# Attention stage: the low parts of q and k and the high and low parts of v are made by VectorE instead of GpSimd

## The chip, the cores and the metric

The kernel runs on one core of a Trainium2 chip. The metric is the device time of one launch in microseconds (us), as the median of several runs. Engines are named as the profile names them: PE is TensorE, PEld its weight loads, DVE is VectorE, ACT is ScalarE, POOL is GpSimd, and SP is SyncE, which issues most of the transfers.

## What is computed

One layer of a hybrid encoder, once for a prompt of 1024 tokens and once for 32 sample tokens with a cache of 512 past tokens. The change lies in the attention branch alone:

```python
q, k, v, fl, ga, u, gs = jnp.split(z, [...], axis=-1)         # z = RMSNorm(h) @ w_in
s = jnp.einsum('bthd,bshd->bhts', q, k) * (HEAD_DIM ** -0.5)  # 8 heads of 128
bias = cq[..., :, None] - ck_t[:, :, None, :]                 # cumulated log forget gates
s = jnp.where(kpos <= qpos, s + bias, NEG_INF)
pr = jax.nn.softmax(s, axis=-1)
att = jnp.einsum('bhts,bshd->bthd', pr, v)
mixed = jnp.concatenate([att * silu(ga), ssm * silu(gs)], axis=-1)
h = h + mixed @ w_out
```

All of it is fp32. The kernel makes each fp32 product from three products of rounded parts: a number x is split into a high part (a copy to a rounded type, `F32R`) and a low part (x minus the high part), and high*high, low*high and high*low are accumulated.

## The kernel before

The program is a row of stages, each a block in which the five engines run their own instruction streams and meet only at semaphores: a projection stage, `stage_attention`, a side stage (gated unit and layer embedding), and a post stage with the output projections. No scheduler is at work: each engine executes its stream in the order in which the code was written, and a wait holds all that stands behind it on that engine.

In `stage_attention` the 8 heads come one after the other; heads 0, 1, 6 and 7 are written out, and 2 to 5 run in a loop of two heads a turn. A head has 8 steps. `SLOTS[s]` says which 128-row block of queries a step works on: step 0 has the blocks 0 and 1 (128 and 256 keys), steps 1 to 6 the blocks with 384, 512, 640, 768, 896 and 1024 keys, and step 7 the sample tokens with 544 keys. The chain of one step is:

- PE makes the scores (`scores`, lines 1971 and 2020) into one of two PSUM buffers, two steps ahead of the rest;
- DVE adds the bias and takes the row bound (`bias`, line 2246) into one of four buffers `prob`;
- ACT takes the exponential (`exponentials`, line 2150);
- PE turns the probabilities (`turn_probs`, line 2037; the sample step 2042) into one of two PSUM banks `turned`;
- ACT rounds them to `pt_hi` (`high_parts`, line 2161), and DVE subtracts to get `pt_lo` (`low_parts`, line 2270);
- PE multiplies with v (`weigh`, into `att`, line 1971): queries 0 to 511 at step 5 of the head, queries 512 to 1023 in two halves at step 7 and at step 0 of the next head, the samples at its step 1;
- DVE multiplies `att` with the gate (`gate_out`, line 2280), and a head later with the reciprocal sums (`scale`, line 2262).

In step s of its stream DVE does `bias(s+1)`, then `low_parts(s-1)`, then what else is due: `gate_out` of the last head at steps 1 and 2, `gate_out` of this head at step 6, and at step 7 `low_kc` of the next head, `invert` and `scale`. PE in step s does `scores(s+2)`, one group of transposes for the next head (`turn`, into the one bank `prep`, which ACT copies out by `copy_k`, `copy_v` and `split_kc`), `turn_probs(s)`, and a `weigh` where one is due. Before line 2037 may write a bank, `lo_done` of the group that used this bank last must be there; before a `weigh`, `lo_done` of the last two groups of its queries.

Beside this each head needs its operands in high and low parts, made one head ahead into one of two buffers each. ACT makes `q_hi` and `k_hi` (`split_qk`, line 2119, steps 0 and 1) and `kc_hi`. GpSimd makes the rest in `prepare`, in this order: `k_lo`, `q_lo`, `vc_hi` and `vc_lo` (the cached v), and, once ACT has copied the turned v, `v_hi` and `v_lo`. For head 0 this runs once ahead of everything; for head h+1 it starts when PE has finished the last `weigh` of head h-1 (`weighed[2]`), early in head h.

```python
def prepare(h, b):                      # on GpSimd
    pool.wait_ge(k_hi_done, h + 1)
    sub(k_lo[b][:], k_raw[:], k_hi[b][:], k_lo_done)
    ...
    nc.gpsimd.tensor_copy(v_hi[b][:], v_tok[:]).then_inc(v_hi_done, 1)
    pool.wait_ge(v_hi_done, h + 1)
    sub(v_lo[b][:], v_tok[:], v_hi[b][:], v_lo_done)
```

The semaphores that `prepare` raises are waited for at few places: PE waits for `q_lo_done` and `k_lo_done` ahead of the first scores of a head and for `v_lo_done` ahead of its first `weigh`; ACT waits for `v_lo_done` before it overwrites `v_tok`; SP waits for `k_lo_done`, `q_lo_done`, `vc_hi_done` and `vc_lo_done` before it loads the next `k_raw`, `q_raw`, `kc_raw` and `vc_raw` over the old.

Of the kernel before, what the change touches and what calls it, by code (L numbers as in the profile page):

```python
# [22 lines left out]
F32 = mybir.dt.float32  # L23
# [131 lines left out]
def settle(eng, passed):  # L155

    eng.sem_inc(passed, 1)
# [1596 lines left out]
def stage_attention(nc, d, G):  # L1754
# [15 lines left out]
    with ExitStack() as ctx:  # L1770
# [4 lines left out]
        q_raw, k_raw, v_raw = G["first_raw"]  # L1775
# [61 lines left out]
        def heads(eng, head):  # L1837

            head(0, 0, 0, first=True)
            head(1, 1, 0)  # L1840
            with eng.Fori(1, HEADS // 2 - 1) as i:
                head(i * 2, 0, i)
                head(i * 2 + 1, 1, i)
            head(HEADS - 2, 0, HEADS // 2 - 1)
            head(HEADS - 1, 1, HEADS // 2 - 1, last=True)
# [70 lines left out]
        @block.gpsimd  # L1916
        def _(pool):
            nc.gpsimd.memset(mask_f[:], 0.0)
            nc.gpsimd.memset(mask_s_f[:], 0.0).then_inc(masks_made, 1)
            pool.wait_ge(masks_made, 1)  # L1920

            nc.gpsimd.affine_select(out=mask_f[:], in_=mask_f[:], compare_op=ALU.is_ge, fill=NEG, base=0,
                                    pattern=[[-1, P]], channel_multiplier=1).then_inc(masks_made, 1)
            pool.wait_ge(masks_made, 2)

            r0 = P - T_SAMPLE
            nc.gpsimd.affine_select(out=mask_s_f[r0:], in_=mask_s_f[r0:], compare_op=ALU.is_ge, fill=NEG,
                                    base=0, pattern=[[-1, T_SAMPLE]], channel_multiplier=1) \
                .then_inc(masks_made, 1)
            pool.wait_ge(masks_made, 3)  # L1930
            nc.gpsimd.memset(v_tok[:, TT], 0.0)
            nc.gpsimd.tensor_copy(mask[:], mask_f[:])
            nc.gpsimd.tensor_copy(mask_s[:], mask_s_f[:])
            nc.gpsimd.tensor_copy(ident_bf[:], ident[:]).then_inc(masks_ready, 1)

            def sub(out, a, hi, done):
                nc.gpsimd.tensor_tensor(out, a, hi.bitcast(F32), ALU.subtract).then_inc(done, 1)

            def prepare(h, b):

                pool.wait_ge(k_hi_done, h + 1)
                sub(k_lo[b][:], k_raw[:], k_hi[b][:], k_lo_done)
                pool.wait_ge(q_hi_done, h + 1)
                sub(q_lo[b][:], q_raw[:], q_hi[b][:], q_lo_done)
                pool.wait_ge(c_loaded, h * 32 + 32)
                settle(pool, G["passed"])
                nc.gpsimd.tensor_copy(vc_hi[b][:], vc_raw[:]).then_inc(vc_hi_done, 1)
                pool.wait_ge(vc_hi_done, h + 1)
                sub(vc_lo[b][:], vc_raw[:], vc_hi[b][:], vc_lo_done)
                pool.wait_ge(v_copied, h * 3 + 3)  # L1950
                settle(pool, G["passed"])
                nc.gpsimd.tensor_copy(v_hi[b][:], v_tok[:]).then_inc(v_hi_done, 1)
                pool.wait_ge(v_hi_done, h + 1)
                sub(v_lo[b][:], v_tok[:], v_hi[b][:], v_lo_done)

            prepare(0, 0)

            def head(h, b, i, first=False, last=False):
                if not first:

                    pool.wait_ge(weighed[2], h)
                if not last:
                    prepare(h + 1, 1 - b)
            heads(pool, head)

        @block.tensor
        def _(pe):
            def three(out, pairs, start, stop, lhs, rhs):
# [257 lines left out]
        @block.vector  # L2226
        def _(dve):
            def low_kc(h, b):
                dve.wait_ge(kc_hi_done, h + 1)
                nc.vector.tensor_tensor(kc_lo[b][:], prep[:], kc_hi[b][:].bitcast(F32), ALU.subtract) \  # L2230
                    .then_inc(kc_lo_done, 1)

            def bias(h, s, hb, pair):

                b, it = s % 2, h * 4 + s // 2
                dve.wait_ge(scored[b], it + 1)
                if not isinstance(h, int) or it:
                    dve.wait_ge(exped[b], it)
                if not isinstance(h, int) or it > 1:
                    dve.wait_ge(prob_free[b], h * 4 + (s // 2 - 1))  # L2240
                if s == 0:
                    dve.wait_ge(negc_loaded[hb], pair * 16 + 16)
                settle(dve, G["passed"])
                for n, (t, col) in enumerate(SLOTS[s]):
                    width, row = ((t + 1) * P, 0) if t < TT else (NS, T_PROMPT)
                    z = nc.vector.tensor_tensor_reduce(  # L2246
                        out=prob[s % 4][:, col:col + width], in0=score[b][:, col:col + width],
                        in1=negc[hb][:, row:row + width], scale=-SCALE, scalar=3.0e38, op0=ALU.add, op1=ALU.min,
                        accum_out=stat[b][:, n, 0:1])
                z.then_inc(biased[b], 1)  # L2250

            def invert(h, hb):
                for b in range(2):
                    dve.wait_ge(exped[b], h * 4 + 4)
                if not isinstance(h, int) or h > 1:
                    dve.wait_ge(rec_turned, h - 1)
                nc.vector.reciprocal(rec[hb][:], sums[hb][:]).then_inc(rec_ready, 1)

            def scale(h, hb):
                dve.wait_ge(gated, h * 3 + 3)  # L2260
                dve.wait_ge(rec_loaded, h * 32 + 32)
                nc.vector.tensor_tensor(mix[hb][:], mix[hb][:], rec_bc[:], ALU.mult).then_inc(scaled, 1)

            def low_parts(h, s):
                for n, group in enumerate(GROUPS_OF[s]):
                    gi = first_group[s] + n
                    bank, x = turned[gi % 2], (0 if s < 3 else 1 if s < 7 else 2)
                    dve.wait_ge(hi_done[gi % 2], h * (per_head // 2) + (gi // 2 + 1))
                    for (out, src), (hi, _) in zip(taken(group, pt_lo[x], bank), taken(group, pt_hi[x], bank)):
                        c = nc.vector.tensor_tensor(out, src, hi.bitcast(F32), ALU.subtract)  # L2270
                    c.then_inc(lo_done[gi % 2], 1)

            def gate_out(h, x, hb, pair=None):
                cols = slice(512 * x, 512 * x + (512 if x < 2 else T_SAMPLE))
                dve.wait_ge(weighed[x], h + 1)
                if x == 0:
                    if not isinstance(pair, int) or pair:
                        dve.wait_ge(mix_stored[hb], pair * 16)
                    dve.wait_ge(gate_loaded[hb], pair * 16 + 16)
                nc.vector.tensor_tensor(mix[hb][:, cols], att[:, 0:cols.stop - cols.start], gate[hb][:, cols],  # L2280
                                        ALU.mult).then_inc(gated, 1)

            dve.wait_ge(masks_ready, 1)
            low_kc(0, 0)
            bias(0, 0, 0, 0)

            def head(h, hb, i, first=False, last=False):
                for s in range(8):
                    if s < 7:
                        bias(h, s + 1, hb, i)  # L2290
                    elif not last:
                        bias(h + 1, 0, 1 - hb, i + hb)
                    if first and s == 1:
                        for n in range(4):
                            dve.wait_ge(G["sem"][f"z_put{n}"], put_count(2 * NP - 1))
                    if s > 0:
                        low_parts(h, s - 1)
                    elif not first:
                        low_parts(h - 1, 7)
                    if s == 1 and not first:  # L2300
                        gate_out(h - 1, 1, 1 - hb)
                    if s == 2 and not first:
                        gate_out(h - 1, 2, 1 - hb)
                    if not last and s == 7:
                        low_kc(h + 1, 1 - hb)
                    if s == 6:
                        gate_out(h, 0, hb, i)
                    if s == 7:
                        invert(h, hb)
                        if not first:  # L2310
                            scale(h - 1, 1 - hb)
            heads(dve, head)
            low_parts(HEADS - 1, 7)
            gate_out(HEADS - 1, 1, 1)
            gate_out(HEADS - 1, 2, 1)
            scale(HEADS - 1, 1)
# [676 lines left out]
```

## Time and profile before

| | |
|---|---|
| median of 3 runs | 2404.68 us (2404.39 to 2406.39) |
| the profiled execution: its own time, its span | 2403.17 us, 2401.5 us |
| busy over the span: PE, PEld, DVE, ACT, POOL | 93%, 88%, 64%, 33%, 11% |
| granted TensorE clock, mean | 0.979 of full speed |
| attention stage | about 1192 to 1415 us of the span |

The trace gives for each instruction its start and its length, and in brackets how long its engine had sat idle just before it and which instruction on which engine released it. Lengths of neighbours can overlap by a few hundredths of a us, since an engine starts the next instruction while the last one drains. An idle time costs something only if an engine that sets the end waits behind it. The view of stretches gives the busy time of each engine between two moments.

### The profile page before, as it was taken

What the parts mean: (1) busy time and instruction counts of PE and PEld (TensorE: products, weight loads), DVE (VectorE), ACT (ScalarE), POOL (GpSimd) and SP (SyncE); (2) the same over time, 40 slices, a digit from 0 to 9 for tenths busy, and PEclk for the clock granted to TensorE, in tenths of its full rate; (3) what the DMA queues carried; (4) which work ended last, traced back from release to release, by engine and by line L of the source; (5) the groups of instructions that cost most, each with busy time, mean ns of one, the idle gap of its engine ahead of it and who ended that gap; (6) DMA issues with size and microseconds to landing.
All of it is one profiled execution on the core that took longest, in us unless ns stands there. A gap on an engine that the chain in (4) does not pass through costs nothing. (4 is left out here: it accounts for less than half of the span.)

```text
span 2401.5 us, 43214 instructions
## 1 busy us (share of the span) xinstructions
PE 2240.1 (93%) x15969; PEld 2114.6 (88%) x15969; DVE 1539.9 (64%) x2827; ACT 791.0 (33%) x1669; POOL 274.4 (11%) x334
## 2 busy tenths in 40 slices
PE   3999999999899999999799978979999999999996
PEld 3999999999899999999778868967888879999996
DVE  6778766766787788886356646654446666445554
ACT  6542333333533333334366636220001112001112
POOL 0011000000111111211244400000001110001110
PEclk9999999999999999999899989989999999999998
DMA  8484444444757878875376655454445436443442
GB/s 243 147 255 110 141 136 124 150 132 130 283 179 206 237 213 228 232 223 169 124 234 203 200 181 181 127 166 127 114 145 147 113 106 217 111 111 112 110 111 96
DMA packets 401861, 394.65 MB, mean 164 GB/s; under 512 B 75248, under 2 KB 343128, under 8 KB 395248
## 3 DMA queue, kind: packets, MB, share of 16 engines
q1 hardware_dynamic: 353344, 267.24, 38.8%
q0 software_dynamic: 20704, 77.95, 9.8%
q10 hardware_dynamic: 27664, 47.49, 6.1%
q8 instruction: 92, 1.51, 0.3%
q14 instruction: 57, 0.47, 0.1%
HBM read 261.88 MB, written 122.05 MB: 160 GB/s over the span
## 5 line engine op out<-in xcount | busy, mean ns | idle before, releaser
L758 PE MATMUL acc<-t_act,w_hi 128*128 128x264 f32 x5376 | 887.8, 287 | 12.0 <-ACT acc L979 4.1
L758 PEld LDWEIGHTS acc<-t_act,w_hi 128*128 128x128 f32 x5376 | 748.3, 189 | 18.7 <-issue 17.3
L758 PE MATMUL acc<-t_act,w_lo 128*128 128x264 f32 x2688 | 548.3, 285 | 0.0
L2700 PE MATMUL post_acc<-region_hi,w_post_hi 128*128 128x272 f32 (+1 forms) x1536 | 418.0, 326 | 24.3 <-DVE region_lo L2809 19.6
L758 PEld LDWEIGHTS acc<-t_act,w_lo 128*128 128x128 f32 x2688 | 417.4, 189 | 0.0
L2700 PE MATMUL post_acc<-region_hi,w_post_lo 128*128 128x272 f32 (+1 forms) x1536 | 415.0, 324 | 0.0
L2700 PE MATMUL post_acc<-region_lo,w_post_hi 128*128 128x272 f32 (+1 forms) x1536 | 414.4, 324 | 0.0
L2700 PEld LDWEIGHTS post_acc<-region_hi,w_post_hi 128*128 128x128 f32 x1536 | 257.7, 189 | 50.3 <-issue 16.6
L1313 DVE TENSOR_TENSOR w_lo<-w_raw_f,w_hi 128x512 fp32r<-128x512 f32 x288 | 198.0, 687 | 144.3 <-ACT w_hi L968 144.0
L2700 PEld LDWEIGHTS post_acc<-region_lo,w_post_hi 128*128 128x128 f32 x1536 | 258.0, 189 | 22.1
L2700 PEld LDWEIGHTS post_acc<-region_hi,w_post_lo 128*128 128x128 f32 x1536 | 256.7, 189 | 22.8
L968 ACT CAST w_hi<-w_raw_f 128x512 fp32r<-128x512 f32 x288 | 177.9, 618 | 267.3 <-PE acc L758 245.6
L142 DVE TENSOR_TENSOR w_post_lo<-w_raw,w_post_hi 128x1024 fp32r<-128x1024 f32 x128 | 150.5, 1216 | 0.0
L2817 DVE TENSOR_TENSOR total<-post_acc,side 128x512 f32<-128x512 f32 (+1 forms) x32 | 22.6, 708 | 183.4 <-PE post_acc L2700 183.4
L2740 ACT CAST region_hi<-total 128x512 f32 (+1 forms) x32 | 20.4, 636 | 330.7 <-DVE total L2817 319.0
L137 DVE CAST w_post_hi<-w_raw 128x1024 fp32r<-128x1024 f32 x128 | 114.2, 930 | 9.5 <-DMA w_raw<-in_w_out_dram 8.5
L2835 DVE TENSOR_TENSOR h<-h,gate_sig 128x512 f32<-128x512 f32 (+1 forms) x32 | 22.7, 709 | 117.1 <-ACT gate_sig L2747 117.1
L2754 ACT ACTIVATE junk<-y_ps 128x128 f32<-128x128 f32 (+1 forms) x144 | 37.0, 274 | 174.3 <-PE y_ps L2685 174.3
L2651 POOL TENSOR_TENSOR total<-region_hi,region_lo 128x512 f32 (+3 forms) x32 | 50.3, 1575 | 293.1 <-DVE h L2838 285.0
L649 POOL DMA_DIRECT2D zT<-zb x80 | 43.3, 542 | 345.6 <-DVE zb L1329 147.5
L2246 DVE CUSTOM_DVE_ANT_0 prob<-score,negc_bc 128x128 f32<-128x128 f32 (+8 forms) x72 | 53.5, 752 | 32.8 <-PE score L2020 32.5
L2270 DVE TENSOR_TENSOR pt_lo<-turned,pt_hi 128x512 fp32r<-128x512 f32 (+2 forms) x112 | 52.8, 507 | 28.5 <-ACT pt_hi L2161 27.1
(382 smaller groups left out, 3084.9 us busy)
## 6 DMA issues: line engine op xcount, KB each, us to landing
w_raw_f<-in_w_in_dram SPq DMA_DIRECT2D x96, 512.0 KB, 4.1
w_raw<-in_w_out_dram SPq DMA_DIRECT2D x64, 512.0 KB, 4.8
w_raw<-in_w_pg_dram SPq DMA_DIRECT2D x64, 512.0 KB, 4.7
cT<-zb SPq DMA_DIRECT2D x24, 1056.0 KB, 4.7
zb<-cT POOLq DMA_DIRECT2D x96, 264.0 KB, 6.0
zT<-zb POOLq DMA_DIRECT2D x80, 264.0 KB, 3.6
eT<-e_out ACTq DMA_DIRECT2D x16, 528.0 KB, 3.1
t_act<-tS POOLq DMA_DIRECT2D x7, 1056.0 KB, 10.6
```

The costliest lines, as they stand in the source:

```text
L137: nc.vector.tensor_copy(self.hi[b][:, h * self.kh:(h + 1) * self.kh], self.raw[h][:]) \
L142: nc.vector.tensor_tensor(self.lo[b][:, part], self.raw[h][:], self.hi[b][:, part].bitcast(F32), ALU.subtract).then_inc(self.split[h], 1)
L649: pool.dma_start(d["zT"][row:row + P, tok:tok + HN], zb[b][:, i]).then_inc(z_put[i], 16)
L758: mm = pe.matmul(out[:, c, 0:QN], w[:, k, :], t_act[:, SIDE[r], x, k, c * QN:(c + 1) * QN], start=(opens and k == 0 and m == 0), stop=(k = ...
L968: nc.scalar.copy(w_hi[n % RING_W][:], factor(p, r)).then_inc(hi_done, 1)
L1313: TT_(w_lo[n % RING_W][:], factor(n // 7, n % 7), w_hi[n % RING_W][:].bitcast(F32), ALU.subtract) \
L2246: z = nc.vector.tensor_tensor_reduce(out=prob[s % 4][:, col:col + width], in0=score[b][:, col:col + width], in1=negc[hb][:, row:row + widt ...
L2270: c = nc.vector.tensor_tensor(out, src, hi.bitcast(F32), ALU.subtract)
L2651: nc.gpsimd.tensor_tensor(total[b][:, 0:WIDTH[part]], row(hi, part, m).bitcast(F32), row(lo, part, m).bitcast(F32), ALU.add).then_inc(tota ...
L2700: mm = pe.matmul(acc[b][:, c, 0:width], w[:, k, :], a[region][:, k, start:start + width], start=(k == 0 and n == 0), stop=(k == KD - 1 and ...
L2754: s = nc.scalar.activation(junk[0:rows, t], tr_ps[b][0:rows, t * P:(t + 1) * P], ACT.Square, accum_out=ssq[0:rows, t, bass.ds(m, 1)])
L2835: nc.vector.tensor_tensor(h2[b][:, 0:w], h2[b][:, 0:w], sig[b][:, 0:w], ALU.mult).then_inc(e_gated, 1)
```

## The change

The six operations of `prepare` leave GpSimd and go to VectorE, as four pieces: `low_k`, `low_q`, `split_vc` and `split_v`. GpSimd keeps only the making of the masks. Nothing else is edited; the operands, their buffers and their semaphores are the same.

```diff
-            def prepare(h, b):
-                ...
-            prepare(0, 0)
-
-            def head(h, b, i, first=False, last=False):
-                if not first:
-                    pool.wait_ge(weighed[2], h)
-                if not last:
-                    prepare(h + 1, 1 - b)
-            heads(pool, head)
...
+            def sub(out, a, hi, done):
+                nc.vector.tensor_tensor(out, a, hi.bitcast(F32), ALU.subtract).then_inc(done, 1)
+
+            def low_k(h, b):
+                dve.wait_ge(k_hi_done, h + 1)
+                sub(k_lo[b][:], k_raw[:], k_hi[b][:], k_lo_done)
+
+            def low_q(h, b):
+                dve.wait_ge(q_hi_done, h + 1)
+                sub(q_lo[b][:], q_raw[:], q_hi[b][:], q_lo_done)
+
+            def split_vc(h, b):
+                dve.wait_ge(c_loaded, h * 32 + 32)
+                settle(dve, G["passed"])
+                nc.vector.tensor_copy(vc_hi[b][:], vc_raw[:]).then_inc(vc_hi_done, 1)
+                dve.wait_ge(vc_hi_done, h + 1)
+                sub(vc_lo[b][:], vc_raw[:], vc_hi[b][:], vc_lo_done)
+
+            def split_v(h, b):
+                dve.wait_ge(v_copied, h * 3 + 3)
+                settle(dve, G["passed"])
+                nc.vector.tensor_copy(v_hi[b][:], v_tok[:]).then_inc(v_hi_done, 1)
+                dve.wait_ge(v_hi_done, h + 1)
+                sub(v_lo[b][:], v_tok[:], v_hi[b][:], v_lo_done)
+
             dve.wait_ge(masks_ready, 1)
+            low_k(0, 0)
+            low_q(0, 0)
             low_kc(0, 0)
             bias(0, 0, 0, 0)
+            split_vc(0, 0)
+            split_v(0, 0)
...
                     if s == 2 and not first:
                         gate_out(h - 1, 2, 1 - hb)
+                    if not last:
+                        if s == 2:
+                            if not first:
+                                dve.wait_ge(weighed[2], h)
+                            low_k(h + 1, 1 - hb)
+                        if s == 3:
+                            low_q(h + 1, 1 - hb)
+                        if s == 4:
+                            split_vc(h + 1, 1 - hb)
+                        if s == 6:
+                            split_v(h + 1, 1 - hb)
                     if not last and s == 7:
                         low_kc(h + 1, 1 - hb)
                     if s == 6:
                         gate_out(h, 0, hb, i)
```

How DVE's stream stands at three places, before and after. `ISA prob,stat` is a `bias`, `ISA stat` the reading of its row bound; line numbers of the changed kernel are 30 lower around here.

DVE at the start of the stage, ahead of head 0, before:

```order
L2230 TENSOR_TENSOR kc_lo<-prep,kc_hi 128x512
L2246 ISA prob,stat<-score,negc_bc 128x128
L2246 ISA stat 128x1
L2246 ISA prob,stat<-score,negc_bc 128x256
L2246 ISA stat 128x1
L2246 ISA prob,stat<-score,negc_bc 128x384
```

and after:

```order
L2254 TENSOR_TENSOR k_lo<-k_raw,k_hi 128x1056
L2254 TENSOR_TENSOR q_lo<-q_raw,q_hi 128x1056
L2200 TENSOR_TENSOR kc_lo<-prep,kc_hi 128x512
L2216 ISA prob,stat<-score,negc_bc 128x128
L2216 ISA stat 128x1
L2216 ISA prob,stat<-score,negc_bc 128x256
L2216 ISA stat 128x1
L2267 CAST vc_hi<-vc_raw 128x512
L2254 TENSOR_TENSOR vc_lo<-vc_raw,vc_hi 128x512
L2274 CAST v_hi<-v_tok 128x1152
L2254 TENSOR_TENSOR v_lo<-v_tok,v_hi 128x1152
L2216 ISA prob,stat<-score,negc_bc 128x384
```

Two subtractions now stand ahead of `kc_lo`, and four operations stand between the bias of step 0 and that of step 1.

DVE in a head, from the last `gate_out` of the head before (step 2) to the bias of 1024 keys (step 5), before:

```order
L2280 TENSOR_TENSOR mix<-att,gate 128x32
L2246 ISA prob,stat<-score,negc_bc 128x768
L2246 ISA stat 128x1
L2270 TENSOR_TENSOR pt_lo<-turned,pt_hi 128x4x128
L2246 ISA prob,stat<-score,negc_bc 128x896
L2246 ISA stat 128x1
L2270 TENSOR_TENSOR pt_lo<-turned,pt_hi 128x4x128
L2270 TENSOR_TENSOR pt_lo<-turned,pt_hi 128x128
L2246 ISA prob,stat<-score,negc_bc 128x1024
```

and after:

```order
L2254 TENSOR_TENSOR k_lo<-k_raw,k_hi 128x1056
L2216 ISA prob,stat<-score,negc_bc 128x768
L2216 ISA stat 128x1
L2240 TENSOR_TENSOR pt_lo<-turned,pt_hi 128x4x128
L2254 TENSOR_TENSOR q_lo<-q_raw,q_hi 128x1056
L2216 ISA prob,stat<-score,negc_bc 128x896
L2216 ISA stat 128x1
L2240 TENSOR_TENSOR pt_lo<-turned,pt_hi 128x4x128
L2240 TENSOR_TENSOR pt_lo<-turned,pt_hi 128x128
L2267 CAST vc_hi<-vc_raw 128x512
L2254 TENSOR_TENSOR vc_lo<-vc_raw,vc_hi 128x512
L2216 ISA prob,stat<-score,negc_bc 128x1024
```

Each of the three biases has work for the next head directly ahead of it.

DVE in a head, from the `low_parts` of 896 keys (step 6) to that of 1024 keys (step 7), before:

```order
L2270 TENSOR_TENSOR pt_lo<-turned,pt_hi 128x4x128
L2270 TENSOR_TENSOR pt_lo<-turned,pt_hi 128x3x128
L2280 TENSOR_TENSOR mix<-att,gate 128x512
L2246 ISA prob,stat<-score,negc_bc 128x128
L2246 ISA stat 128x1
L2246 ISA prob,stat<-score,negc_bc 128x256
L2246 ISA stat 128x1
L2270 TENSOR_TENSOR pt_lo<-turned,pt_hi 128x4x128 x2
```

and after:

```order
L2240 TENSOR_TENSOR pt_lo<-turned,pt_hi 128x4x128
L2240 TENSOR_TENSOR pt_lo<-turned,pt_hi 128x3x128
L2274 CAST v_hi<-v_tok 128x1152
L2254 TENSOR_TENSOR v_lo<-v_tok,v_hi 128x1152
L2250 TENSOR_TENSOR mix<-att,gate 128x512
L2216 ISA prob,stat<-score,negc_bc 128x128
L2216 ISA stat 128x1
L2216 ISA prob,stat<-score,negc_bc 128x256
L2216 ISA stat 128x1
L2240 TENSOR_TENSOR pt_lo<-turned,pt_hi 128x4x128 x2
```

The split of v stands ahead of the gate, of the first bias of the next head and of the `low_parts` of 1024 keys.

## Rows read from the trace of the kernel before

**Rows 1.** Stretches, one loop head: length, busy us of each engine, granted clock, DMA
```profile
core 0: us, PE busy (x) PEld busy (x) DVE busy (x) ACT busy (x) POOL busy (x), PEclk, DMA share, GB/s
1315.85:1341.92 26.07, 24.16 (x167) 21.14 (x167) 16.52 (x39) 17.32 (x43) 10.51 (x7) 1.00 0.67 217
```

**Rows 2.** Timeline, DVE in a loop head: start, us, instruction, [idle before <-releaser]
```profile
1315.73 0.19 DVE L2280 TENSOR_TENSOR mix<-att,gate 128x32 f32<-128x32 f32 x1 [0.61 <-PE att L1971]
1317.24 0.96 DVE L2246 CUSTOM_DVE_ANT_0 prob<-score,negc_bc 128x768 f32<-128x768 f32 x1 [1.32 <-PE score L2020]
...
1319.21 1.09 DVE L2246 CUSTOM_DVE_ANT_0 prob<-score,negc_bc 128x896 f32<-128x896 f32 x1 [0.19 <-PE score L2020]
...
1321.15 0.89 DVE L2270 TENSOR_TENSOR pt_lo<-turned,pt_hi 128x512 fp32r<-128x512 f32 x2 [0.84 <-ACT pt_hi L2161]
1322.28 1.23 DVE L2246 CUSTOM_DVE_ANT_0 prob<-score,negc_bc 128x1024 f32<-128x1024 f32 x1 [0.24 <-PE score L2020]
...
1323.59 1.02 DVE L2270 TENSOR_TENSOR pt_lo<-turned,pt_hi 128x512 fp32r<-128x512 f32 x2
1324.53 0.71 DVE L2246 CUSTOM_DVE_ANT_0 prob<-score,negc_bc 128x544 f32<-128x544 f32 x1
...
1326.61 1.16 DVE L2270 TENSOR_TENSOR pt_lo<-turned,pt_hi 128x512 fp32r<-128x512 f32 x2 [1.36 <-ACT pt_hi L2161]
1328.15 0.69 DVE L2280 TENSOR_TENSOR mix<-att,gate 128x512 f32<-128x512 f32 x1 [0.38 <-PE att L1971]
1329.12 0.29 DVE L2246 CUSTOM_DVE_ANT_0 prob<-score,negc_bc 128x128 f32<-128x128 f32 x1 [0.28 <-PE score L2020]
...
1330.35 1.29 DVE L2270 TENSOR_TENSOR pt_lo<-turned,pt_hi 128x512 fp32r<-128x512 f32 x2 [0.58 <-ACT pt_hi L2161]
```

**Rows 3.** Timeline, ACT and PE in the same loop head
```profile
1321.65 1.07 ACT L2150 ACTIVATE prob<-prob,stat 128x896 f32<-128x896 f32 x1
1324.86 1.15 ACT L2150 ACTIVATE prob<-prob,stat 128x1024 f32<-128x1024 f32 x1
1331.77 0.50 PE L1971 MATMUL att<-pt_hi,v_hi 128*128 128x512 f32 x1 [0.19 <-DVE pt_lo L2270]
```

**Rows 4.** Single lines, DVE splits elsewhere: ns min/median/max, first and last start, shape
```profile
L137 DVE CAST w_post_hi<-w_raw x128: 635/686/1861, 1599.2 to 2355.4; 128x1024 fp32r<-128x1024 f32 x128
L137 DVE CAST w_glu_s_hi<-w_glu_s_raw x16: 419/423/440, 1492.0 to 1567.9; 128x512 fp32r<-128x512 f32 x16
L142 DVE TENSOR_TENSOR w_glu_s_lo<-w_glu_s_raw,w_glu_s_hi x16: 682/685/718, 1492.6 to 1568.8; 128x512 fp32r<-128x512 f32 x16
L2493 DVE TENSOR_TENSOR y_lo<-y_raw,y_hi x8: 1251/1252/1259, 1449.8 to 1498.2; - x6, 128x1056 fp32r<-128x1056 f32 x2
```

**Rows 5.** Timeline, start of the stage: DVE, ACT, PE
```profile
1206.83 0.56 DVE L2246 CUSTOM_DVE_ANT_0 prob<-score,negc_bc 128x384 f32<-128x384 f32 x1 [0.52 <-PE score L2020]
...
1207.43 0.62 ACT L2150 ACTIVATE prob<-prob,stat 128x384 f32<-128x384 f32 x1
...
1208.60 0.54 ACT L2161 CAST pt_hi<-turned 128x128 fp32r<-128x128 f32 x2 [0.46 <-PE turned L2037]
...
1210.66 0.66 PE L1990 MATMUL prep<-ident,k_raw 128*128 128x128 f32 x4 [1.03 <-ACT k_tok L2125]
```

**Rows 6.** Timeline, head 0: DVE and ACT
```profile
1218.37 1.23 DVE L2246 CUSTOM_DVE_ANT_0 prob<-score,negc_bc 128x1024 f32<-128x1024 f32 x1 [0.25 <-PE score L2020]
...
1225.82 1.29 DVE L2270 TENSOR_TENSOR pt_lo<-turned,pt_hi 128x512 fp32r<-128x512 f32 x2 [0.67 <-ACT pt_hi L2161]
...
1220.29 1.18 ACT L2150 ACTIVATE prob<-prob,stat 128x1024 f32<-128x1024 f32 x1
```

**Rows 7.** Timeline: DVE casts beside a POOL addition; `k_lo` on POOL; last head's bias
```profile
1817.63 2.38 DVE L137 CAST w_post_hi<-w_raw 128x1024 fp32r<-128x1024 f32 x2
...
1817.92 1.54 POOL L2651 TENSOR_TENSOR total<-region_hi,region_lo 128x512 f32 x1 [10.31 <-DVE h L2838]
...
1315.85 2.47 POOL L1937 TENSOR_TENSOR k_lo<-k_raw,k_hi 128x1056 fp32r<-128x1056 f32 x1 [10.72 <-PE att L1971]
...
1394.26 0.96 DVE L2246 CUSTOM_DVE_ANT_0 prob<-score,negc_bc 128x768 f32<-128x768 f32 x1 [1.31 <-PE score L2020]
```

More of the change, by code:

```diff
@@ L1934, in _ @@
             nc.gpsimd.tensor_copy(ident_bf[:], ident[:]).then_inc(masks_ready, 1)
-            def sub(out, a, hi, done):
-                nc.gpsimd.tensor_tensor(out, a, hi.bitcast(F32), ALU.subtract).then_inc(done, 1)
-            def prepare(h, b):
[L1941 to L1954, printed above, removed]
-            prepare(0, 0)
-            def head(h, b, i, first=False, last=False):
-                if not first:
-                    pool.wait_ge(weighed[2], h)
-                if not last:
-                    prepare(h + 1, 1 - b)
-            heads(pool, head)
         @block.tensor
```

## The prediction

> **What bounds the kernel now.** I read the table of stretches first, one loop head at a time [rows 1]: in 26.07 us PE is busy for 24.16, DVE for 16.52, ACT for 17.32, POOL for 10.51, at the full granted clock. So the stage is PE's, with 1.9 us of PE waits a head, and a faster engine for the splits can give back no more than those. POOL's 10.5 us hide beside PE: nothing in the rows of PE waits for them. What to see next is where DVE's 9.5 us of idle lie, for it is not one hole: from step 2 to step 7 the timeline shows nine small ones of 0.19 to 1.36 us, between operations that other engines wait for [rows 2]. Third, who waits for DVE at once: at step 7 PE starts the weighing of queries 512 to 1023 at 1331.77, released by `pt_lo` [rows 3], whose two operations ended at 1330.35 + 1.29 = 1331.64 [rows 2]. Whatever delays that `low_parts` delays PE one for one. The other places have ACT between DVE and PE, with some margin.
>
> **Prices on DVE.** No split of q, k or v stands on DVE in this trace; the same operations on the same types do elsewhere [rows 4]. A subtraction of 128x1056 takes 1.252 us and one of 128x512 0.685, so 1.04 ns an element, and 1.352 us for the 1152 of `v_lo`. A cast of 512 takes 0.423 and of 1024 0.686 in the median, 0.514 ns an element: 0.752 us for `v_hi`. That is 1.25 + 1.25 + 0.42 + 0.69 + 0.75 + 1.35 = 5.7 us a head, and DVE comes to 22.2 of 26 us. Neighbours on DVE overlap by about 0.08 us (1323.59 + 1.02 = 1324.61, next start 1324.53) [rows 2], which I take off, but not between a high part and its low part, where DVE waits for itself; there I put a gap of 0.05 (an estimate; from no gap to 0.1).
>
> **Start of the stage.** `low_k` and `low_q` of head 0 cost nothing: they fall into the time in which PE and ACT hand each other the turned k and v. `split_vc` and `split_v` do cost. DVE ends the bias of step 0 at 1206.83 - 0.52 = 1206.31 [rows 5] and then does 0.42 + 0.69 + 0.75 + 1.35 with two gaps and two overlaps, to about 1209.4; the bias of step 1 started at 1206.83 [rows 5] and is 2.6 late. ACT's exponential of step 1 started at 1207.43, right behind that bias; it goes to 1210.05. Behind it on ACT stand the first `pt_hi`, which had 0.46 us of idle to give [rows 5], `k_hi` of head 1 and the copy of its turned k, and for that copy PE already waited 1.03 us at 1210.66 [rows 5]. So 2.6 less about 0.5: **+2.1 us** on PE, from 1.5 (no gaps, more slack on ACT) to 2.9.
>
> **Steps 2 to 4 of a head.** `k_lo` takes 1.25 us in the hole of 1.32 ahead of the bias of 768 keys [rows 2]: nothing. `q_lo` pushes the bias of 896 keys from 1319.21 by 0.9; it is done at 1321.2, before ACT takes it up at 1321.65 [rows 3], and the idle of 0.84 ahead of the next `pt_lo` [rows 2] swallows it. `vc_hi` and `vc_lo` (1.1 us less overlap, 0.24 of idle) push the bias of 1024 keys by 0.75, to end at 1324.25; ACT takes it up at 1324.86 [rows 3]: nothing. The `pt_lo` behind it is 0.6 late, the bias of 544 keys too, and the idle of 1.36 at 1326.61 [rows 2] ends it. **0**, with margins of some 0.45 and 0.6 us on ACT.
>
> **Step 6.** From the `pt_lo` at 1326.61 to that at 1330.35 DVE has three holes, 0.38 + 0.28 + 0.58 = 1.24 us [rows 2]. `v_hi` starts at 1327.69 and ends at 1328.44, `v_lo` runs from 1328.49 to 1329.84, the gate from 1329.76 to 1330.45, the two small biases to about 1331.0; `pt_lo` starts there instead of at 1330.35. What was the last thing before (`pt_hi` from ACT, with 0.58 of idle on DVE) is now early, and DVE is last: **+0.6 us** a head on PE, from 0.4 (the gate's own hand-overs overlap more) to 0.9 (no overlap at all). It is paid in heads 1 to 6, since head 7 prepares nothing: 3.6 us, from 2.4 to 5.4. After PE's weighing everything keeps its place relative to PE, so nothing earns it back within the head.
>
> **Head 0** has no `gate_out` of an earlier head, no `scale` and no storing of sums, and ACT runs closer behind DVE there: the exponential of 1024 keys started at 1220.29, 0.69 us after its bias had ended (1218.37 + 1.23 = 1219.60) [rows 6], against 1.35 in a loop head (1324.86 less 1323.51) [rows 2, 3]. The same walk puts that bias 1.3 late relative to the rest, so here exponential, `pt_lo` and PE's transposes are about 1 us late, and the split of v comes on top: the `pt_lo` of 1225.82 with its 0.67 of idle [rows 6] is **1.5 us** late beyond the start's 2.1; from 0.6 (as a loop head) to 2.4.
>
> **Waits and queues.** The new waits of DVE (`k_hi_done`, `q_hi_done`, `c_loaded`, `v_copied`, `weighed[2]`) are all for work that is done when DVE comes by: POOL did each of these operations earlier than or at the place where DVE will do it, save `v_hi`, where ACT's last small copy of v stands before DVE's `pt_lo` ends. Behind each wait stand the biases and `pt_lo`; that is the order that I walked. On SP, the loads of `k_raw`, `q_raw`, `kc_raw` and `vc_raw` wait for the same semaphores; `k_lo` and `q_lo` come no later than before, and the cached v is loaded behind PE's turning of the cached k at step 6 anyway. Those operands are used a head later: 0.
>
> **Sum.** 2.1 + 1.5 + 3.6 = 7.2 us on the profiled execution's 2403.17 (its span of 2401.5 and 1.7 around it) gives 2410.4; the median of the runs lies 1.5 above that execution, so the forecast for the median is **2411.9 us**, +0.3%. The stage ends with all engines meeting, so what is lost in it moves the end.
>
> **Rivals.** All of it hidden but the start. What speaks for it is DVE's idle sum, 9.5 us against 5.7. The place is the hole at step 6: if ACT's `pt_hi` or PE's transposes come 0.6 us later relative to DVE than in the rows, or the split of v takes 1.3 us instead of 2.1, `pt_lo` is again released by ACT and a head costs nothing. Then 2404.7 + 2.1 = 2406.8, and with head 0 too 2408.3; this ends not slower by the bound of 0.2% (4.8 us), which is about what a measurement of this kernel can tell from no change. Against it: the hole is 1.24 us by the rows. 28%.
>
> Faster, since GpSimd lets the memory go. Casts on DVE do suffer beside POOL: a pair that overlaps a POOL addition took 2.38 us [rows 7], against a median of 0.686 each, and the longest single one took 1.861 [rows 4]. If DVE's biases and subtractions in this stage suffered alike, POOL's leaving would shorten them; all of PE's waits being owed to that would give 7 x 1.9 = 13.3, less the start's 2.1, so 2393.5 at the best, and it needs more than half of this to pass 0.2%. Against it: the bias of 768 keys took 0.96 us [rows 2] while POOL made `k_lo` at 1315.85 to 1318.32 [rows 7], and in the last head, where POOL has nothing, also in 0.96 [rows 7]. The stage has no casts on DVE before. 4%. The Trainium skill (GPSIMD Engine Reference, Key points) states that GpSimd shares its SBUF interfaces with VectorE, with contention for instructions in a 2-port mode or with two SBUF inputs. By that rule this change would free DVE; the casts of the post stage agree, and the biases of this stage, with their scores in PSUM, show nothing of it.
>
> Heavier. If DVE hands over slower than I count (gaps of 0.1, no overlap), or casts run at the subtraction's rate (`v_hi` 1.2 instead of 0.75), ACT's margins of 0.45 and 0.6 at steps 3 and 4 are used up and a head costs 1.2 us instead of 0.6: 2.9 + 2.2 + 6 x 1.2 = 12.3, so 2417.0. The 1.861 in the row of casts speaks for it, but it stands beside POOL work that is gone here. 10%.
>
> That the change does something else than it says is excluded by the order of instructions: POOL has no arithmetic left in the heads, and DVE has six operations more for each.
>
> **How the numbers follow.** The forecast (a cost above 4.8 and below 11) gets 58%, hidden 28%, heavier 10%, faster 4%. Slower by over 0.2%: 58 + 10 = 68%; within 0.2%: 28%; faster: 4%. The range reaches down to the start alone, 2406.8, and up to the heavier case at 2417.0, with half a us on each side.
>
> **What would show it.** In the new trace: POOL without a row between the masks and the side stage; the bias of step 1 some 2.6 us after the bias of step 0 instead of 0.6; about 26.7 us from head to head instead of 26.07, with PE's busy time unchanged at 24.2; at step 7 a PE wait of some 0.8 us released by `pt_lo`, and that `pt_lo` without idle ahead of it; unchanged intervals in steps 2 to 5. `v_hi` near 0.75 us and `v_lo` near 1.35. Heads of 26.07 us would prove the step 6 term wrong; waits of ACT for `stat` at steps 4 and 5 would prove the margins wrong; shorter biases or `pt_lo` would be the memory rival.

## The result and the profile after

The changed kernel takes 2412.28 us (median of 9 runs, 2408.78 to 2413.64) against 2404.83 of the kernel before (9 runs), a ratio of 1.0028 with a 95% interval of 1.0019 to 1.0037: 7.45 us slower by the two medians, where 7.2 were forecast. The profiled execution after took 2412.7 us, its span is 2411.0.

The page's first lines and the stretch of one loop head, from step 2 to step 2, which answers to [rows 1]:

```profile
PE 2244.7 (93%) x15969; PEld 2118.3 (88%) x15969; DVE 1578.8 (65%) x2875; ACT 792.0 (33%) x1669; POOL 190.4 (8%) x286
```
```profile
1321.68:1348.28 26.60, 24.16 (x167) 21.12 (x167) 21.30 (x44) 17.42 (x43) 0.00 (x0) 1.00 0.70 213
```

PE and ACT do the same work as before; POOL's 10.51 us became 4.8 us more of busy time on DVE (the six rows sum to 5.7 us, as priced; where neighbours overlap, busy time counts the moment once), and the head is 0.53 us longer. DVE in that head, answering to [rows 2] (start, us, instruction, idle before it):

```profile
1321.79 1.25 DVE L2254 TENSOR_TENSOR k_lo<-k_raw,k_hi 128x1056 fp32r<-128x1056 f32 x1
1323.20 0.96 DVE L2216 CUSTOM_DVE_ANT_0 prob<-score,negc_bc 128x768 f32<-128x768 f32 x1 [0.17 <-PE score L1990]
...
1324.89 1.25 DVE L2254 TENSOR_TENSOR q_lo<-q_raw,q_hi 128x1056 fp32r<-128x1056 f32 x1
...
1327.11 0.89 DVE L2240 TENSOR_TENSOR pt_lo<-turned,pt_hi 128x512 fp32r<-128x512 f32 x2
...
1328.97 1.22 DVE L2216 CUSTOM_DVE_ANT_0 prob<-score,negc_bc 128x1024 f32<-128x1024 f32 x1
...
1332.58 1.16 DVE L2240 TENSOR_TENSOR pt_lo<-turned,pt_hi 128x512 fp32r<-128x512 f32 x2 [0.81 <-ACT pt_hi L2131]
1333.65 0.75 DVE L2274 CAST v_hi<-v_tok 128x1152 fp32r<-128x1152 f32 x1
1334.43 1.36 DVE L2254 TENSOR_TENSOR v_lo<-v_tok,v_hi 128x1152 fp32r<-128x1152 f32 x1
1335.71 0.68 DVE L2250 TENSOR_TENSOR mix<-att,gate 128x512 f32<-128x512 f32 x1
...
1336.86 1.28 DVE L2240 TENSOR_TENSOR pt_lo<-turned,pt_hi 128x512 fp32r<-128x512 f32 x2
```

`k_lo` leaves 0.17 us of the hole of 1.32. Behind `q_lo` and the cached v DVE runs without a pause until 0.81 us of the hole of 1.36 are still there at 1332.58: up to that point the head is as before. From there to the last `pt_lo` it is 4.28 us, 3.74 before, without any idle. PE right behind (its waits at step 7; first the one of the kernel before at the same place), and ACT's two exponentials of steps 4 and 5, 3.23 us apart as before (3.21 in [rows 3]):

```profile
1331.14 0.43 PE L2042 MATMUL turned<-ident,prob 32*128 32x32 f32 x5 [0.41 <-issue]
```
```profile
1337.65 0.43 PE L2012 MATMUL turned<-ident,prob 32*128 32x32 f32 x5 [0.96 <-issue]
1338.28 0.50 PE L1941 MATMUL att<-pt_hi,v_hi 128*128 128x512 f32 x1 [0.20 <-DVE pt_lo L2240]
```
```profile
1327.60 1.07 ACT L2120 ACTIVATE prob<-prob,stat 128x896 f32<-128x896 f32 x1
...
1330.83 1.15 ACT L2120 ACTIVATE prob<-prob,stat 128x1024 f32<-128x1024 f32 x1
```

The start of the stage, answering to [rows 5], DVE, ACT and PE:

```profile
1207.45 0.42 DVE L2267 CAST vc_hi<-vc_raw 128x512 fp32r<-128x512 f32 x1
...
1210.58 0.55 DVE L2216 CUSTOM_DVE_ANT_0 prob<-score,negc_bc 128x384 f32<-128x384 f32 x1
...
1211.17 0.62 ACT L2120 ACTIVATE prob<-prob,stat 128x384 f32<-128x384 f32 x1 [2.62 <-DVE stat L2216]
1211.19 0.50 PE L1941 MATMUL score<-k_hi,q_hi 128*128 128x512 f32 x1 [1.34 <-DVE stat L2216]
...
1213.82 0.66 PE L1960 MATMUL prep<-ident,k_raw 128*128 128x128 f32 x4 [1.29 <-ACT k_tok L2095]
```

To compare stages I use PE's own rows: the *start* from the first transposition of the stage to the second one of k for head 1 (1194.14 to 1210.66 before, 1195.36 to 1213.82 after); *head 0* from there to the weighing of its step 7 (1227.21; 1231.78); *heads 1 to 6* as a sixth of the way to that weighing in head 6; the *stage* to the last weighing.

| kernel | start | head 0 | heads 1 to 6, each | stage | median us | ratio to before, interval |
|---|---|---|---|---|---|---|
| before | 16.52 | 16.55 | 26.07 | 219.4 | 2404.83 | |
| changed | 18.46 | 17.96 | 26.60 | 225.9 | 2412.28 | 1.0028, 1.0019 to 1.0037 |
| e1 v back on POOL | 17.51 | 17.65 | 26.17 | 222.1 | 2405.2 | 1.0006, 0.9997 to 1.0015 |
| e2 q, k back on POOL | 18.46 | 17.37 | 26.62 | 225.4 | 2409.48 | 1.0022, 1.0013 to 1.0032 |
| e3 early start | 16.82 | 17.97 | 26.64 | 224.5 | 2408.63 | 1.0020, 1.0011 to 1.0029 |
| e4 and v at step 0 | 16.68 | 17.64 | 26.07 | 220.6 | 2404.32 | 1.0002, 0.9993 to 1.0011 |
| e5 POOL busy too | 19.63 | 22.18 | 32.42 | 267.8 | 2452.81 | 1.0202, 1.0188 to 1.0216 |
| e6 one cast more | 19.12 | 19.41 | 27.55 | 233.8 | 2419.63 | 1.0070, 1.0056 to 1.0084 |
| e7 e4, copies first | 17.37 | 17.65 | 25.87 | 222.3 | 2404.98 | 1.0005, 0.9996 to 1.0014 |
| e8 before, copies first | 16.62 | 16.52 | 24.93 | 212.6 | 2398.37 | 0.9980, 0.9971 to 0.9989 |
| e9 e7, cached v at step 1 | 16.13 | 16.82 | 25.03 | 213.7 | 2398.78 | 0.9974, 0.9963 to 0.9985 |

The stage columns are of one execution each. Kernels with the same step 6 agree there within 0.04 us a head (26.60, 26.62 and 26.64 for changed, e2 and e3; 26.07 twice for before and e4), so a difference of 0.1 us a head shows, while one of 2 us in the medians hardly does. The kernel before had medians of 2403.86 to 2404.83 in these comparisons.

### The profile page after: what moved, and what is told of

The parts are those of the page before. It is cut to its first block and busy times, and to the rows that moved or that the text cites. A ratio compares the mean times of both kernels' runs of the same rounds, so it can differ in the third digit from the quotient of the medians.

```text
span 2411.0 us, 43200 instructions
## 1 busy us (share of the span) xinstructions
PE 2244.7 (93%) x15969; PEld 2118.3 (88%) x15969; DVE 1578.8 (65%) x2875; ACT 792.0 (33%) x1669; POOL 190.4 (8%) x286
## 5 line engine op out<-in xcount | busy, mean ns | idle before, releaser
L2757 ACT ACTIVATE gate_sig<-post_acc 128x512 f32<-128x512 f32 (+1 forms) x32 | 19.6, 611 | 149.4 <-PE post_acc L2710 149.2
```

## Experiments: which of the added operations cost

**e1**: v back on GpSimd, the rest as changed.

```diff
+            def prepare(h, b):
+                pool.wait_ge(v_copied, h * 3 + 3)
...
-            split_v(0, 0)
...
-                        if s == 6:
-                            split_v(h + 1, 1 - hb)
```

> The changed kernel with one part undone: GpSimd makes v_hi and v_lo again, VectorE keeps the low parts of q and k and both parts of the cached v (3.6 of the 5.7 us a head). Theory (the cost lies at two places, the start and step 6): with only the cached v between the first two biases the start costs 0 to 0.3 us instead of 1.9; step 6 costs nothing, so heads 1 to 6 go back to 26.07 us from 26.60; head 0 keeps 0.6 to 1.0 us, because its bias of 1024 keys still comes 1.3 late. Sum about +1, near 2405.9 us. Rival (VectorE's added load as such costs, wherever it stands): 3.6/5.7 of 7.4 us, so +4.7, 2409.5 us and heads of 26.4 us.

2405.2 us, and heads of 26.17: without the split of v step 6 costs 0.1 us a head, though DVE keeps 3.6 us of added work. The rival's 26.4 is out. The start was a miss, 1.0 instead of at most 0.3. Two things show in it, the cast of the cached v at twice its length while POOL made `v_lo` (first two rows), and a TensorE clock that rose some 2 us later than in the kernel before (third row, the stretch from 14.0 to 15.0 us after the first transposition, still at 0.50, the 1.2 GHz level; before it was at 1.00 from 14 us on):

```profile
1202.09 2.64 POOL L1937 TENSOR_TENSOR v_lo<-v_tok,v_hi 128x1152 fp32r<-128x1152 f32 x1
1204.19 0.83 DVE L2287 CAST vc_hi<-vc_raw 128x512 fp32r<-128x512 f32 x1
```
```profile
1206.10:1207.10 1.00, 1.00 (x7) 1.00 (x6) 0.82 (x4) 0.71 (x2) 0.00 (x0) 0.50 1.03 364
```

The clock is enough to explain the miss. In e3, e4, e7 and e9, whose DVE order at the start is the same, it rose 13.7, 13.4, 14.9 and 12.0 us after the first transposition, and their starts are 16.82, 16.68, 17.37 and 16.13 us: an estimated 0.43 us of start for each us by which the clock rises later. At e1's 15.2 that makes 17.5, and 17.51 was measured.

**e2**: the counterpart, `k_lo` and `q_lo` back on GpSimd.

```diff
+            def prepare(h, b):
+                pool.wait_ge(k_hi_done, h + 1)
+                sub(k_lo[b][:], k_raw[:], k_hi[b][:], k_lo_done)
+                pool.wait_ge(q_hi_done, h + 1)
+                sub(q_lo[b][:], q_raw[:], q_hi[b][:], q_lo_done)
...
-            low_k(0, 0)
-            low_q(0, 0)
...
-                            low_k(h + 1, 1 - hb)
-                        if s == 3:
-                            low_q(h + 1, 1 - hb)
```

> The other part undone: GpSimd makes the low parts of q and k again, VectorE keeps both parts of v and of the cached v (3.2 of the 5.7 us a head). Theory: the start costs 1.9 us as in the changed kernel, heads 1 to 6 stay at 26.6 us, since step 6 is as it was and steps 2 and 3 cost nothing; head 0 about 1.0 instead of 1.4. Sum about +6.1, near 2411 us. Rival (load as such): 3.2/5.7 of 7.4 us, so +4.2, 2409 us and heads of 26.37 us.

Start 18.46, heads 26.62: as in the changed kernel, with 2.5 us less on DVE. `k_lo` and `q_lo` cost the loop heads nothing; head 0 gives back 0.6.

**e3**: head 0's splits ahead of `low_kc`, where DVE waits for ACT.

```diff
+            split_vc(0, 0)
+            split_v(0, 0)
             low_kc(0, 0)
             bias(0, 0, 0, 0)
-            split_vc(0, 0)
-            split_v(0, 0)
```

> The changed kernel, with the splits of v and of the cached v for head 0 ahead of the low part of the cached k, in the 8 us in which VectorE waits for ACT there, instead of between the first two biases. Theory: the start term of 1.9 us goes (from the first turned k of head 0 to the second of head 1 16.5 us again, not 18.5), head 0 keeps its 1.4 and heads 1 to 6 their 26.60 us; near 2410.3 us. Rival (the late second bias is not what delays PE at the start): no change, 2412.3 us.

The start falls from 18.46 to 16.82, the rest stays. So the late second bias was what delayed PE there. The 0.3 us left to the 16.52 of before is about what the later rise of the clock makes (13.7 against 13.1 us).

**e4**: e3, and v split at step 0 of its own head.

```diff
                     elif not first:
                         low_parts(h - 1, 7)
+                        split_v(h, hb)
...
-                        if s == 6:
-                            split_v(h + 1, 1 - hb)
```

> As the run with the early start, and the split of v for heads 1 to 7 moved from step 6 of the head before to step 0 of its own head, behind low_parts, where VectorE waits about 1.6 us for PE's scores. The same work on VectorE as in the changed kernel. Theory: heads 1 to 6 at 26.07 us, start 0, head 0 0.6 to 1.0: near 2405.8 us. Rival (load as such, or 2.1 us of split cost the same wherever they stand): heads stay near 26.6 us, 2410 us.

Heads of 26.07, the same as before to the hundredth, with all of the added work on DVE. The place costs, not the load. Head 0 keeps 1.1 us (17.64 against 16.55), though its step 6 no longer has a split: so 1.1 of its 1.4 come from steps 2 to 4 and 0.3 from the split of v (17.97 in e3).

**e6**: the reverse, a second cast ahead of each `v_hi`.

```diff
+                nc.vector.tensor_copy(v_lo[b][:], v_tok[:])
                 nc.vector.tensor_copy(v_hi[b][:], v_tok[:]).then_inc(v_hi_done, 1)
```

> The changed kernel with one more cast of 128x1152 ahead of each v_hi (0.67 us net). Theory (VectorE sets the end of step 6 with no slack left): each of heads 1 to 6 grows by 0.67 to 27.27 us, head 0 and the start by the same, about +5.4 over the changed kernel, 2417.7 us. Rival (the time at step 6 is set by ACT or PE and VectorE has slack): less than a third of it.

Heads 2 to 6 grew by 0.68 each (27.32 against 26.64), the start by 0.66: the whole length of the cast. So DVE has no slack left at either place. The total is +7.3 instead of +5.4. Head 0 grew by 0.8 and head 1 by 1.6 more than the cast, and a lower clock lies in both: PE waited 2.47 us for the second bias at 1211.25 and 1.30 at 1213.87, and then the granted clock stood at the 1.2 GHz level for 3 us (the stretch with its clock in the last column but two); it fell once more in head 1 (0.66 from 1233 to 1238), which took 28.71 us. That the waits brought it down was not tried by a run of its own.

```profile
1211.25 0.50 PE L1941 MATMUL score<-k_hi,q_hi 128*128 128x512 f32 x1 [2.47 <-DVE stat L2216]
```
```profile
1213.70:1216.70 3.00, 2.83 (x10) 2.55 (x11) 0.69 (x4) 1.87 (x5) 0.00 (x0) 0.51 0.06 24
```

## Experiments: what GpSimd's leaving is worth, and what PE's other waits are

**e5**: the changed kernel, with GpSimd doing as much arithmetic as before on tiles of its own.

```diff
+            def prepare(h, b):
+                pool.wait_ge(k_hi_done, h + 1)
+                busy(h, T, 3)
...
+                busy_copy(h, 1152, 7)
+                busy(h, 1152, 8)
```

`busy` subtracts and `busy_copy` copies, in the widths and behind the waits of the old `prepare`.

> The changed kernel, and beside it GpSimd does as much arithmetic as before at the same places, on tiles of its own that nobody reads. Theory (GpSimd's arithmetic took nothing from VectorE's biases and subtractions, but holds VectorE's casts, as the cast pair of the post stage shows): biases, pt_lo, k_lo, q_lo keep their lengths to 0.02 us; v_hi, which now meets GpSimd's work on the same 1152 elements, is held and grows from 0.75 to between 1.2 and 2 us, so that heads 1 to 6 grow from 26.6 to 27 to 27.9 us; 2415 to 2420 us. Rival one (no sharing at all in this stage): 2412.3 us and v_hi of 0.75. Rival two (GpSimd takes from every VectorE operation): biases and subtractions longer as well.

2452.81 us, 40 more than the changed kernel and far over my 2415 to 2420. The casts are held as I expected, `v_hi` at 1.34. What I missed is `v_lo`, and with less `q_lo` and `vc_lo` (`v_hi` and `v_lo` in the first two rows; the third is POOL meanwhile, the fourth all eight `v_lo`, min/median/max in ns, the fifth all biases):

```profile
1326.68 1.34 DVE L2312 CAST v_hi<-v_tok 128x1152 fp32r<-128x1152 f32 x1
1328.06 3.68 DVE L2292 TENSOR_TENSOR v_lo<-v_tok,v_hi 128x1152 fp32r<-128x1152 f32 x1
...
1327.49 3.03 POOL L1943 TENSOR_TENSOR idle_c<-idle_a,idle_b 128x1152 f32<-128x1152 f32 x1
...
L2292 DVE TENSOR_TENSOR v_lo<-v_tok,v_hi x8: 1359/3678/3686, 1211.0 to 1426.1; 128x1152 fp32r<-128x1152 f32 x8
...
L2254 DVE CUSTOM_DVE_ANT_0 prob<-score,negc_bc x72: 274/710/1225, 1207.4 to 1450.5; 128x128 f32<-128x128 f32 x8, 128x256 f32<-128x256 f32 x8, 128x384 f32<-128x384 f32 x8, 128x512 f32<-128x512 f32 x8
```

The last row, the biases, stays as in the changed kernel (a median of 715 ns there): operations whose first input lies in PSUM do not notice POOL. A subtraction that reads two SBUF tiles does, but not always; which engine starts first decides. `k_lo` and POOL's first subtraction, in a loop head and then in head 6, the last that prepares:

```profile
1314.00 1.25 DVE L2292 TENSOR_TENSOR k_lo<-k_raw,k_hi 128x1056 fp32r<-128x1056 f32 x1
1314.08 3.48 POOL L1943 TENSOR_TENSOR idle_c<-idle_a,idle_b 128x1056 f32<-128x1056 f32 x1 [16.48 <-PE att L1979]
```
```profile
1410.58 2.46 POOL L1943 TENSOR_TENSOR idle_c<-idle_a,idle_b 128x1056 f32<-128x1056 f32 x1 [15.26 <-PE att L1979]
1410.64 3.51 DVE L2292 TENSOR_TENSOR k_lo<-k_raw,k_hi 128x1056 fp32r<-128x1056 f32 x1
```

Whoever came second stood until about the end of the first, and the first took its usual time (1.25 us on DVE in the changed kernel, 2.45 on POOL in the kernel before). In heads 1 to 5, where the two start within 0.1 us of each other, `k_lo` takes 1.25 us and POOL's subtraction 3.48 to 3.57. `v_lo` fits: it started 0.57 us behind POOL's subtraction, which ended at 1330.52, and 1330.52 + 1.36 is 1331.88, 0.14 past its end. So do the casts here (`v_hi` behind POOL's copy) and the `vc_hi` of e1, which ended 0.29 us after POOL's `v_lo`. In the loop head of the kernel before, all of DVE's work beside POOL had an input in PSUM. Of the 5.8 us by which a head grew, 2.9 are `v_hi` and `v_lo`, and 1.2 `q_lo` and the cached v; the granted clock was 0.95 over a head, which takes a part, and the rest I did not split.

The Trainium skill (GPSIMD Engine Reference, Key points) names contention with VectorE instructions in a 2-port mode or with two SBUF inputs; the run agrees for two SBUF inputs, and in which mode the casts ran no row shows. The prices of [rows 4] held in the changed kernel, where POOL is idle. What is dear is such operations of both engines side by side, not a half move as such: in e1 and e2, which are half moves, the rows of DVE's splits show it once (the `vc_hi` of 0.83 us in e1), and both took less than the whole move.

**e8**: the kernel before, ACT's copies of k and v ahead of its sums and transfers.

```diff
-                    if s == 2 and not first:
-                        copy_rec(h - 1)
-                    if s == 4 and not first:
-                        load_rec(h - 1)
...
                         if s < 3:
                             copy_k(h + 1, s)
                         elif s < 6:
                             copy_v(h + 1, s - 3)
...
+                    if s == 2 and not first:
+                        copy_rec(h - 1)
+                    if s == 4 and not first:
+                        load_rec(h - 1)
```

> The kernel before, with ACT's copies ahead of its row of sums and its transfers, as in the run with copies first, splits on GpSimd. Theory: heads of about 25.2 us, near 2399.5 us; it tells whether the gain of that order needs the splits on VectorE (it should not, the two edits meet on different engines). Rival: no change, 2404.8 us.

**e7**: the same edit on e4.

> As the run with the split of v at step 0, and ACT copies the turned k and v out ahead of its row of reciprocal sums and the issue of its transfers (steps 2 and 4), not behind them. Theory: PE's 1.9 us of waits a head that stayed are ACT's, 0.41 at step 2 and 0.89 at step 4; ACT's copies come 0.4 and 0.5 us earlier, heads 1 to 6 go to about 25.2 us; near 2400.5 us, under both kernels. Rival (something else is last there, such as PE's own work or pt_lo): heads near 26 us, 2405 us.

e8 gains 5.5 us, heads of 24.93. e7 gains next to nothing, heads of 25.87 instead of 26.07 and a start lengthened by the late clock. Views of waits from 1210 to 1380 us, e4 and then e8 (us in total, times, longest), then two of e7 and a row of PE in it:

```profile
PE prep L1960 <- ACT v_tok L2105: 4.6, 6, 0.9
```
```profile
PE prep L1990 <- ACT v_tok L2135: 1.7, 7, 0.2
```
```profile
PE turned L2007 <- DVE pt_lo L2239: 4.6, 7, 0.8
PE prep L1960 <- ACT v_tok L2105: 1.7, 7, 0.2
```
```profile
1327.41 0.96 PE L2007 MATMUL turned<-ident,prob 128*128 128x128 f32 x7 [0.65 <-DVE pt_lo L2239]
```

ACT's lateness went in both (4.6 to 1.7), but in e7 PE then waited at step 5 for `pt_lo` (seven waits, 4.6 us; one of 0.7 in e4, in head 0), which stands behind the split of the cached v: the 0.6 us by which that `pt_lo` is late had been covered by ACT's late copy. My expectation that the two edits do not meet was wrong.

**e9**: e7, the cached v split at step 1 of its own head.

```diff
                         gate_out(h - 1, 1, 1 - hb)
+                        split_vc(h, hb)
...
-                        if s == 4:
-                            split_vc(h + 1, 1 - hb)
```

> As the run with the split of v at step 0 and ACT's copies first, and the split of the cached v for heads 1 to 7 moved from step 4 of the head before to step 1 of its own head, behind the gate. VectorE does the same work as in the changed kernel. In the run without this move PE waited 0.65 us for pt_lo at step 5. Theory (what took the place of ACT's late copies is VectorE at step 5, held by the split of the cached v at step 4): that wait goes, heads 1 to 6 go from 25.87 to 25.1 to 25.3 us, so 3.5 to 4.5 us less than that run and near the kernel before with copies first, 2400 to 2401 us. Rival (q_lo at step 3, or VectorE's load as such, is what holds step 5): heads stay above 25.6 us.

2398.78 us, heads of 25.03, and no wait for `pt_lo` at step 5 among PE's waits. With the same VectorE work as the changed kernel it is some 13 us faster than that by the medians, and faster than the kernel before by 0.26%; e8, with the splits still on GpSimd, is as fast within the intervals. Both beat both kernels; the gain over the kernel before is ACT's order, not the move to VectorE.

## Why the prediction was right, step by step

- **The bound and the last wait** (PE, and `pt_lo` at step 7): right; e1, e4 and e6 show it from three sides. The profile writes PE's wait differently than I said: 0.96 us ahead of the sample's transpositions, marked as issue, where 0.8 released by `pt_lo` was forecast. The same bank stands behind it: before, PE waited 0.41 us at that place, and both times it went on 0.79 us after the start of the two `pt_lo` (1330.35 to 1331.14; 1336.86 to 1337.65).
- **Prices**: `v_hi` 0.75 and `v_lo` 1.36 us, from 0.752 and 1.352; the self-wait gap is 0.03 us, taken as 0.05.
- **Start**: +1.94 for 2.1; e3 takes 1.6 of it away. The path is the one named: ACT's exponential of step 1 comes 15.81 us after the first transposition instead of 13.29, so 2.5 late (2.6 forecast), and from there to PE's transposition behind the copy it is 2.65 instead of 3.23 us (0.5 forecast to be won back, 0.6 measured). PE's wait of 1.34 us for the second bias I had not named; it ends before the one for ACT's copy and adds nothing to it.
- **Steps 2 to 4**: 0 in loop heads, as forecast (e2). With ACT faster it is no longer 0 (e7).
- **Step 6**: +0.53 a head for 0.6, in six heads 3.2 for 3.6; the gate and the biases behind the split closed up a little more.
- **Head 0**: +1.41 for 1.5, by the path named, with 1.1 of it ahead of step 6 as e4 shows (about 1 forecast); two rows of the changed kernel show DVE last there, ahead of ACT and of PE's transposes:

```profile
1224.12 1.15 ACT L2120 ACTIVATE prob<-prob,stat 128x1024 f32<-128x1024 f32 x1 [0.27 <-DVE stat L2216]
...
1224.83 0.95 PE L2007 MATMUL turned<-ident,prob 128*128 128x128 f32 x7 [0.65 <-DVE pt_lo L2240]
```

- **Sum**: the stage is 6.5 us longer in the two profiles, for 7.2. The spans differ by 9.5: 1.2 lie before the stage, where the granted clock in the first 60 us was 0.79 against 1.00, and the rest behind it; I did not look for their cause, and the medians, 7.45 apart, have an interval of 4.6 to 8.9. That 7.45 lies so near to 7.2 is in part luck; the terms above, each within 0.2 us (the six heads together 0.4), are what bears the prediction out.
- **Rivals**: nothing was hidden at step 6, nothing got faster. The memory rival failed for the reason given: no operation of DVE beside POOL was of the kind that suffers, and the bias of 768 keys takes 0.96 us before and after. But I had priced it from casts alone. A fall of the clock behind the new waits of PE was not among my rivals; it stayed away in the changed kernel, with waits of 1.34 and 1.29 us, and came in e6, behind waits of 2.47 and 1.30.

## What to carry to other kernels

Idle time of an engine is worth something only hole by hole: in a loop head 9.5 us of VectorE idle took 5.7 us of work at no cost in one order (e4) and at 0.5 us in another. Put work behind what others wait for, and walk the row of instructions from hole to hole until the delay is used up. And a zero that rests on another engine being late (ACT, here) ends when that engine is mended.

## What had not been expected of the hardware

VectorE and GpSimd hold each other up where VectorE casts or reads two SBUF tiles, and the one that starts second pays: `k_lo` took 1.25 us where it came 0.08 us ahead of GpSimd's subtraction, which then took 3.48 instead of 2.45, and 3.51 us where it came 0.06 behind. The granted clock of TensorE rose at the stage's start between 12.0 and 15.2 us after its first transposition, from kernel to kernel in one execution each, and with one order of VectorE's work there the start went from 16.13 to 17.37 us with it. In e6 it fell again right after waits of PE of 2.5 and 1.3 us; no run shows whether they are the cause.
